# Experts of a hybrid block: value buffers beside the stored gate matrix, row accumulators on its ground, row uses 1.5 steps later

## The reference, cut to what matters

```python
def _peer_ffn(x, w_q, sub_keys, expert_u, expert_v):
    # ... per token: 8 heads choose 16 experts each of 128 * 128, with softmax gates
    def chunk(args):
        xc, ic, gc = args
        u = jnp.take(expert_u, ic, axis=0)
        act = jax.nn.gelu(jnp.einsum('cd,cjd->cj', xc, u), approximate=False) * gc
        return jnp.einsum('cj,cjd->cd', act, jnp.take(expert_v, ic, axis=0))
```

## Time and profile before

| | |
|---|---|
| runs, median | 4627.26 us |
| profiled execution, own time | 4622.6 us |
| its span | 4620.8 us |
| TensorE busy | 4239.9 us (92%) |
| VectorE busy | 3205.6 us (69%) |
| ScalarE busy | 1551.6 us (34%) |
| POOL busy | 703.8 us (15%) |
| granted TensorE clock, mean | 0.964 |
| moved by DMA | 1182 MB, 256 GB/s over the span |

### The profile page before, as it was taken

How to read it: one execution, slowest core, us unless ns; L and a number is a source line. 1 busy time by engine, 2 the same in 40 slices (tenths; PEclk the granted TensorE clock), 3 DMA queues, 4 the chain that set the end, 5 groups by cost and what they waited for, 6 DMA issues and landing times. The chain is left out here.

```text
span 4620.8 us, 61806 instructions
## 1 busy us (share of the span) xinstructions
PE 4239.9 (92%) x23132; PEld 3774.3 (82%) x23132; DVE 3205.6 (69%) x4943; ACT 1551.6 (34%) x2801; POOL 703.8 (15%) x627
## 2 busy tenths in 40 slices
PE   8999989979987989699977799999999999999994
PEld 6888855656767778587767799999999999999993
DVE  4444436746623644589457688898889999888997
ACT  2212213434431421222346333333333333333331
POOL 0000001123320000033620111111111111111110
PEclk9999989989999999799989899999999999999997
DMA  9999976775545549736537999999999999999995
GB/s 283 315 311 313 317 203 198 242 197 177 178 117 194 189 154 298 226 126 189 173 116 202 307 316 323 318 310 317 310 315 314 314 317 313 314 314 309 319 304 182
DMA packets 575824, 1182.07 MB, mean 256 GB/s; under 512 B 63432, under 2 KB 327472, under 8 KB 520784
## 3 DMA queue, kind: packets, MB, share of 16 engines
q1 hardware_dynamic: 505408, 809.55, 57.3%
q0 software_dynamic: 53120, 358.64, 21.5%
q10 hardware_dynamic: 17040, 10.49, 0.8%
HBM read 1009.07 MB, written 228.15 MB: 268 GB/s over the span
## 5 line engine op out<-in xcount | busy, mean ns | idle before, releaser
L102 PE MATMUL h_ps<-xs,h_ut 128*128 128x352 f32 x6144 | 1077.1, 324 | 36.4 <-DVE h_ut L96 36.4
L102 PE MATMUL h_ps<-h_a,h_v 128*128 128x352 f32 x6144 | 1081.2, 324 | 18.7 <-DVE h_a L96 10.9
L102 PEld LDWEIGHTS h_ps<-xs,h_ut 128*128 128x128 f32 x6144 | 1009.9, 188 | 36.9 <-DVE h_ut L96 36.9
L102 PEld LDWEIGHTS h_ps<-h_a,h_v 128*128 128x128 f32 x6144 | 1004.5, 189 | 28.3 <-DVE h_a L96 17.9
L102 PE MATMUL a_ps<-xt_hi,a_w 128*128 128x512 f32 x1792 | 553.1, 390 | 8.1 <-DVE a_w L96 8.1
L96 DVE TENSOR_TENSOR h_v<-h_v_raw,h_v 128x512 fp32r<-128x512 f32 x512 | 350.1, 684 | 73.6 <-ACT h_v L95 73.5
L102 PEld LDWEIGHTS a_ps<-xt_hi,a_w 128*128 128x128 f32 x1792 | 337.0, 188 | 78.5 <-issue 8.3
L95 ACT ACTIVATE h_v<-h_v_raw 128x512 fp32r<-128x512 f32 x512 | 318.2, 622 | 224.4 <-PE h_ps L102 224.3
L102 PE MATMUL a_ps<-xt_lo,a_w 128*128 128x512 f32 x896 | 349.1, 390 | 0.0
L2611 DVE SCALAR_TENSOR_TENSOR y_first<-h_rows,h_acts,y_first 128x2048 f32<-128x2048 f32 x128 | 300.1, 2345 | 0.0
L2605 DVE CUSTOM_DVE_ANT_0 h_rows<-h_rows,h_x_first 128x2048 f32<-128x2048 f32 x128 | 292.2, 2283 | 0.0
(11 more groups left out here) (355 smaller groups left out, 6663.7 us busy)
## 6 DMA issues: line engine op xcount, KB each, us to landing
h_v_raw<-in_peer_v SPq DMA_DIRECT2D x128, 1024.0 KB, 9.0
h_u_raw<-turned_d SPq DMA_DIRECT2D x144, 512.0 KB, 9.4
a_raw<-in_w_in SPq DMA_DIRECT2D x28, 2048.0 KB, 12.4
a_xin<-in_peer_u SPq DMA_DIRECT2D x224, 256.0 KB, 7.8
turned_d<-a_xin SPq DMA_DIRECT2D x56, 1024.0 KB, 6.8
raw_d<-in_peer_u SPq DMA_DIRECT2D x448, 128.0 KB, 4.2
h_u_raw<-raw_d SPq DMA_DIRECT2D x112, 512.0 KB, 8.7
yt_last<-sums_d SPq DMA_DIRECT2D x125, 176.0 KB, 4.5
```

Source lines behind the costliest of these rows:

```text
L102: mm = pe.matmul(out, lhs[a], rhs[b], start=(first and n == 0), stop=(last and n == 2))
```

## The change

What it does, part by part:
- v_raw is allocated on the left side and no longer on grid_last's ground. SP issues both first value loads before the loop, right behind the fourth u half.
- y_first and y_few are allocated on the right side, on grid_last's ground. Their two memsets move from VectorE, behind its first three u splits, to POOL, behind the wait for the store and ahead of the first gather; VectorE's first row use waits for them.
- EARLY_STEPS is 4: SP waits for the store a step later, and issues that step's u halves ahead of this wait instead of at the end of the step.
- LATE_USES is 22: row uses begin six quarters later. The list SLOTS stays, counted from there; in every fourth group of sixteen quarters slot 14 is used too (41 rows in four groups).

```diff
-    EARLY_STEPS, LATE_USES, SPLIT = 3, 16, DENSE - P
+    EARLY_STEPS, LATE_USES, SPLIT = 4, 22, DENSE - P
-        v_raw = [sb(f"v_raw{r}", [P, GRP, Q * P], side="right") for r in range(VR)]
+        v_raw = [sb(f"v_raw{r}", [P, GRP, Q * P]) for r in range(VR)]
...
         def uses_at(n):
-            n -= LATE_USES
-            return n // 16 * 10 + SLOTS.index(n % 16) if n >= 0 and n % 16 in SLOTS and n < Q * STEPS else None
+            g, z = divmod(n - LATE_USES, 16)
+            slots = SLOTS + (14,) * (g % 4 == 3)
+            r = len(SLOTS) * g + g // 4 + slots.index(z) if g >= 0 and z in slots else None
+            return r if r is not None and r < 2 * JOBS else None
...
+            def load_us(s):
+                for h in range(2 * s + 4, 2 * s + 6):
+                    if h < 2 * STEPS:
+                        load_u(h)
...
             load_u(3)
+            for t in range(VR):
+                load_v(t)
             for s in range(last):
-                if s == EARLY_STEPS - 1:
+                early = s == EARLY_STEPS - 1
+                if early:
+                    load_us(s)
                     sp.wait_ge(last_stored, 16)
...
-                t = s - GRP + 2
-                if s >= GRP - 2 and t < STEPS:
-                    if t >= VR:
-                        sp.wait_ge(v_lo, Q * (t - VR) + Q)
+                t = s - GRP + VR
+                if VR <= t < STEPS:
+                    sp.wait_ge(v_lo, Q * (t - VR) + Q)
                     load_v(t)
-                for h in range(2 * s + 4, 2 * s + 6):
-                    if h < 2 * STEPS:
-                        load_u(h)
+                if not early:
+                    load_us(s)
...
                 if r == 0:
                     dve.wait_ge(x1_in, 16 + 16 * FOLD)
+                    dve.wait_ge(cleared, len(y_fetch))
...
-            for y in y_fetch:
-                dve.memset(y[:, :], 0.0).then_inc(cleared, 1)
-            dve.wait_ge(cleared, 2)
...
             pool.wait_ge(last_stored, 16)
             pool.wait_ge(a_gated, EARLY_STEPS)
+            for y in y_fetch:
+                pool.memset(y[:, :], 0.0).then_inc(cleared, 1)
...
-        y_fetch = [ctx.enter_context(nc.sbuf_tensor(f"y_{n}", [P, D], F32)) for n, _ in widths]
+        y_fetch = [ctx.enter_context(nc.sbuf_tensor(f"y_{n}", [P, D], F32, side="right")) for n, _ in widths]
```

## The result

The changed kernel takes 4696.7 us (median of 4 runs, 4690.49 to 4707.0), the kernel before 4627.96 in the same runs: ratio 1.0154, 95% interval 1.0141 to 1.0167, 69 us slower. 4670 was forecast, 4632 to 4705 as the range. The profiled execution is the longest of the four, 4707.0 us with a span of 4705.0, so the traces differ by 84.2 us and the medians by 69.

The account below looks back on a forecast made before the run. TensorE was taken as the bound, with VectorE and the DMA engines close behind. Boundary +64, clock +5, start -20 and end -6 gave +43 on 4627: 4670 us, range 4632 to 4705.

Parts of the forecast that it names:

- step 1: At 30 group boundaries, row uses ahead of VectorE's chain make TensorE wait longer for hidden values: +64 us.
- step 2: Behind TensorE's longer boundary waits the granted clock sometimes falls: +5 us, between 0 and 48.
- the 2.17 us row: A TensorE gap in the trace before, with no clock loss behind it: by it no boundary pays for the clock.
- rival B: The clock falls at each group boundary, by the skill's rule: 4713 us, chance 0.06.
- step 3: At the experts' start the 25.9 us hole and its restart go, some loads come late: -20 us.
- step 4: From quarter 512 to the last three copies, six row uses stand instead of ten: -6 us.
- A: TensorE finds its hidden values in time at group boundaries, leaving only start and end: 4601 us, chance 0.13.
- D: Part of the boundary stalls is taken up, about 0.9 us each left: no change, 4627 us, chance 0.05.
- C: The load burst behind the store only moves from u half 8 to 12: 4685 us, chance 0.11.

Follow-up runs that it names:

- slots_only: The kernel before with only the new places of the row uses (22 quarters late, extra slot in every fourth group): 4712.2 us, ratio 1.0184.
- slot9_to_15: The changed kernel with one slot of ten moved from 9 to 15, its row use going from quarter 15 to quarter 5: 4621.1 us, ratio 0.9996.
- after_deferred: The changed kernel with the fourth part of each group boundary's y product issued behind the next u product on TensorE: 4638.4 us, ratio 1.0029.
- slot9_to_8: The changed kernel with slot 9 moved to 8, its row use going from quarter 15 to quarter 14: 4739.9 us, ratio 1.0253.

## Why the prediction was right

**The boundary (step 1, the row slots).** The mechanism and its place were right, and slots_only, slot9_to_15 and after_deferred each show it from another side. Its size was a little low: waits of 2.8 to 3.0 us in the groups with a value row in quarter 15 and 2.3 to 2.5 with a u row (2.56 and 2.1 in the idle column by my sum), in blocks of four groups as the extra slot turns the parity. The lags were about 0.2 us larger than by my sum: the chain starts 4.7 to 5.0 us behind the boundary with a value row (4.47 forecast) and 4.2 to 4.4 with a u row (4.05). With a few longer ones (3.43 at 2627, 4.67 at 3680, 3.54 at 4205) the idle column has some 82 us from quarter 32 to 496 where before it had 9: +73 instead of +64. The last two of these stand behind groups with the extra row in quarter 4, in which VectorE also waited 1.2 to 1.8 us for raw u halves. I had said that the extra row costs nothing and had not asked when those halves land; at these two boundaries one or both of them cost up to 1.9 us, and no run separates them. And 7 boundaries had no wait before, not 8, which is worth 0.5 us.

**The clock (step 2) was mis-sized.** I took +5 us, reasoning that the work ahead of our gaps is dense. Taking from each of the 29 spacings of two boundaries (quarters 32 to 496) the 62.04 us of matmuls, the wait and 0.2 us of restart, 24 us are left over, in 14 of them 1.2 to 2.9 us, in the others nothing. Of the 13 waits of 2.3 to 2.5 us 3 are followed by a loss, of the 16 of 2.8 us and more 11. In slot9_to_8, with waits of 2.8 to 3.7 us, it is 25 of 29 spacings and 46 us; in after_deferred, with most waits at 0.4 to 1.1, it is 3 spacings and 6 us. The Trainium skill ("TensorE: Matmul & The Clock Gate", HAM oscillation) describes a loop that goes idle in each pass and pays for the clock in each. Here about half of the passes paid, so that case is nearer to this loop than the 2.17 us row that I held against it: rival B was half true. My own sign for it, a granted clock under 0.99, stands in the trace: 0.98 from 2600 to 3500 us.

Which boundaries lose the clock changes from run to run: in slots_only 14 of 29 spacings lose 26 us, others than in the changed kernel. In both kernels the longer a run, the lower its granted clock: 0.965, 0.964, 0.961 and 0.959 at 4690, 4693, 4701 and 4707 us, and 0.963, 0.961, 0.959 and 0.958 at 4699, 4709, 4716 and 4726 us in slots_only. So the clock is the likely reason for the scatter of 17 and 27 us in these two kernels; in slot9_to_8, where nearly all boundaries pay, it is 3 us. Other reasons are not excluded: the kernel before, with hardly a wait, scatters over 13 us too in all its runs of this study.

**The start (step 3)** came close to the number, -18.7 against -20, and with the transfers that I had named: the store landed at 2560 where the run began 6 us late, and u half 12 was the late transfer, 22.5 us. The number is in part luck. The two waits sum up to 4.9 us where the 25.5 MB at 321 to 325 GB/s gave 7, and the clock behind them cost some 3 us, which I had in the bounds of this term and not in its middle.

**The end (step 4)** was wrong in its result, -1.1 against -6, and right in its parts: the chain ended at P(512) + 5.4 (5.9 forecast), six rows stood there, but behind the wait of 3.80 us (1.59 before) 63 matmuls took 13.16 us and later 60 took 11.41, 3.0 and 1.7 us more than 0.162 us each: the clock again.

**The sum.** The medians differ by +69 against +43 forecast. The traces, with the changed kernel's longest run, differ by 84, 41 more than forecast: in the steady stretch 19 us of clock and 9 of waits, 5 at the end (again clock), 1 at the start, and 6 ahead of the experts, which belong to the run. Nothing cancelled; every term came out on the slow side, the clock most of all (24 us in the steady stretch and some 5 at the end instead of 5 in all), and 4697 lies near the upper ends of 4700 and 4705.

The rivals: A (the boundary does not bite) and D needed waits under 0.9 us; the median was near 2.8. C (the start gives nothing) is refuted by the start's -18.7. The version that beats both kernels keeps the early loads and puts the row uses back on their quarters: 4598 us, 0.9950 of the kernel before.

## What to carry to other kernels

A hand-written list of slots carries a phase: its free slots may stand where another engine needs a result at once, and moving the list by a number that is not a multiple of the period turns them away. Work out the lag of the queue at that one instruction, not its mean load; VectorE had 10% of idle time in the kernel before, and in the changed one TensorE waited 2.3 us or more for it at each of thirty boundaries. And where TensorE waits this long once in each pass, count the clock with the wait: it was 24 of the 98 us that the steady stretch lost here.

## What the runs showed of the hardware

- Between stretches of dense matmuls 3 of 13 waits of TensorE of 2.3 to 2.5 us lowered the granted clock to 0.50, and 11 of 16 of 2.8 to 4.7 us did; a fall cost 1.2 to 2.9 us. At the start of the experts a wait of 2.12 us lowered it too.
- POOL's memset of 2048 elements took 1.81 us; VectorE did not wait for it. Behind each row use with a u row VectorE's next u split waited 0.7 to 1.1 us for ScalarE.
- The 8 MB store beside 4.3 MB more of loads landed in 54.0 us instead of 41.4, with 320 and 313 GB/s moved in all over these times.
